# Two lent row slots with a continuous junction, and projections that begin with half of the modulation

## What is computed

```python
mod = silu(c) @ w_ada + b_ada                       # 1024 -> 6 * 1024
sh1, sc1, gt1, sh2, sc2, gt2 = split(mod, 6)
h = rms_norm(x, g_mix) * (1 + sc1) + sh1
q_sb, k_sb, v_sb, q_d, k_d, v_d, gate_sb, gate_d = split(h @ w_in)
# stick-breaking and dilated attention, their outputs gated and merged:
x = x + gt1 * (merged @ w_out)
h2 = rms_norm(x, g_ffn) * (1 + sc2) + sh2
# sparse feed-forward: 8 heads pick 16 of 16384 experts for each token
act = gelu(einsum('cd,ckd->ck', h2, peer_u[expert]))
x = x + gt2 * einsum('ck,ckd->cd', gate * act, peer_v[expert])
x = rms_norm(x, g_final)
# the second block follows: projections, spatial gating, attention, a dense feed-forward layer of 4096
```

## Time and profile before

| | us |
|---|---|
| three runs | 1466.15, 1467.89, 1471.02 |
| median | 1467.89 |
| the profiled execution | 1470.94 |
| its span | 1469.1 |
| PE busy in the span | 1312.6 (89%) |
| DVE busy | 777.3 (53%) |
| ACT busy | 331.3 (23%) |
| POOL busy | 296.4 (20%) |
| read from HBM | 516.89 MB |

### The profile page before, as it was taken

One profiled execution on the slowest core, in us unless ns is written; L12 is line 12 of the kernel. 1 busy time (PEld: TensorE's weight loads), 2 busy tenths in 40 slices (PEclk: granted clock), 3 DMA queues, 4 the chain that ended last, 5 costly groups with the idle time before them and its releaser, 6 DMA issues.

```text
span 1469.1 us, 14710 instructions
## 1 busy us (share of the span) xinstructions
PE 1312.6 (89%) x4900; PEld 748.0 (51%) x4900; DVE 777.3 (53%) x2083; ACT 331.3 (23%) x871; POOL 296.4 (20%) x275
## 2 busy tenths in 40 slices
PE   7999999698998897768888999898886899999997
PEld 6877995464655564334344543444332334554444
DVE  5146535576677677668756676575656522210002
ACT  1231223222221123233213212021110133411102
POOL 1000001333333334332313223232233000000000
PEclk7999999899999999998999999999999999999999
DMA  8966875899999999998999999999999899688882
GB/s 353 409 226 253 305 261 201 348 381 379 389 403 418 418 417 410 420 410 332 417 390 417 390 419 416 411 411 377 418 417 417 337 365 350 214 260 277 286 304 103
DMA packets 101594, 518.91 MB, mean 353 GB/s; under 512 B 11665, under 2 KB 12561, under 8 KB 66705
## 3 DMA queue, kind: packets, MB, share of 16 engines
q0 software_dynamic: 38592, 293.62, 49.0%
q1 hardware_dynamic: 61632, 220.43, 40.7%
q10 hardware_dynamic: 1296, 3.93, 0.7%
HBM read 516.89 MB, written 1.05 MB: 353 GB/s over the span
## 4 chain that ended last, share of the span: by engine, by line
PE 58%; DMA 29%; DVE 8%; ACT 3%; issue 2%; POOL 0%; DVEq 0%; ACTq 0%; POOLq 0%
PE ps_M L921 24%; DMA ring<-in_w_second 15%; DMA ring<-in_peer_uv,arena 8%; PE ps_T L718 7%; PE ps_T L719 6%; PE ps_M L450 5%; DMA ring<-in_w_pq 4%; PE ps_M L628 4%; DVE ring L1994 2%; PE ps_M L687 2%; PE ps_M L460 1%; PE ps_M L651 1%; DVE arena L1790 1%; PE ps_SA L687 1%; DMA arena<-in_w_ada 1%
## 5 line engine op out<-in xcount | busy, mean ns | idle before, releaser
L921 PE MATMUL ps_M<-ring,arena 128*128 128x512 f32 x1072 | 495.3, 601 | 39.8 <-DMA ring<-in_w_second 38.2
L921 PEld LDWEIGHTS ps_M<-ring,arena 128*128 128x128 f32 x1072 | 194.2, 190 | 288.9 <-issue 232.6
L1211 POOL DMA_INDIRECT ring<-in_peer_uv,arena x145 | 164.6, 1135 | 368.5 <-PE ps_T L719 324.6
L1211 POOL DMA_INDIRECT arena<-in_peer_uv,arena x111 | 124.8, 1124 | 328.3 <-PE ps_T L719 240.7
L718 PE MATMUL ps_T<-ring,arena 128*128 128x512 f32 x246 | 132.6, 621 | 36.9 <-ACT arena L1347 36.7
L1336 ACT ACTIVATE arena<-arena 128x2 f32<-128x2 f32 x128 | 26.0, 203 | 474.8 <-DVE arena L2014 471.3
L719 PE MATMUL ps_T<-ring,arena 128*128 128x512 f32 x246 | 129.2, 608 | 0.0
L718 PE MATMUL ps_T<-arena 128*128 128x512 f32 x190 | 100.0, 608 | 24.1 <-ACT arena L1347 24.1
L1994 DVE SCALAR_TENSOR_TENSOR ring<-ring,arena 128x1024 f32<-128x1024 f32 x72 | 87.6, 1220 | 58.4 <-DMA ring<-in_peer_uv,arena 58.1
L1994 DVE SCALAR_TENSOR_TENSOR ring<-ring,merged 128x1024 f32<-128x1024 f32 x73 | 89.1, 1221 | 48.2 <-DMA ring<-in_peer_uv,arena 48.1
L719 PE MATMUL ps_T<-arena 128*128 128x512 f32 x190 | 97.8, 596 | 0.0
(11 more groups left out here) (284 smaller groups left out, 1452.6 us busy)
## 6 DMA issues: line engine op xcount, KB each, us to landing
ring<-in_w_second SPq DMA_DIRECT2D x276, 512.0 KB, 4.5
ring<-in_w_in SPq DMA_DIRECT2D x70, 512.0 KB, 7.4
arena<-in_w_ada POOLq DMA_DIRECT2D x12, 2048.0 KB, 10.9
ring<-in_w_pq SPq DMA_DIRECT2D x30, 512.0 KB, 4.5
ring<-in_w_out SPq DMA_DIRECT2D x16, 512.0 KB, 4.8
ring<-in_w_br SPq DMA_DIRECT2D x16, 384.0 KB, 3.5
ring<-in_peer_uv,arena POOLq DMA_INDIRECT x145
arena<-in_rel SPq DMA_DIRECT2D x1, 2048.0 KB, 10.5
```

The source lines that it names most:

```text
L921: m = mm(bank, left[c], w[:, c, :], start=first and c == 0, stop=last and c == 1)
L1211: pool.indirect_dma_start(row_slots[n % PAIRS], None, A["peer_uv"], bass.IndirectOffsetOnAxis(ap=expert[:, u % 3, k:k + 1], axis=0))\
```

## The change

**Row slots.** tmp and merged are lent as row slots 3 and 4 to the gathers below 63 (`EARLY`); the ring pairs are slots 5 to 8. The order of slots is 0, 1, 2, 3, 4, 5, 7, 8, 6 below 63 and 0, 1, 2, 5, 7, 8, 6 from there on (`CYCLES`); each gather waits for the row that its slot held (`ROW_SLOT`). The tiles before the first turns are reordered (q0, ldv, lsv, q1), and PE does ldv's values, then the two gates ("lga", 0) and ("lgb", 0), then lsv's values, all before turn 0; ACT's takes and stick_soft1(0) move along, lsv's copy to turn 4.

**Junction.** `due(n)` goes on over row 127: rows 126 and 127 are accumulated in turns 128 and 129, and residual(0) follows these two turns. `LEAD` is 8. gate_expo and gate_norm of a head are done in turns 12 and 14 of the head before (head 0's before turn 0), and the product with the spatial mask moves from turn (7, 0) to (6, 13).

**Opening.** The chunks are loaded and worked in the order 0, 2, 1, 3 (`CHUNKS`). PE takes two blocks of chunks 0 and 2 and none of 1 and 3. The normalised tmp, the gain and hT are made in two halves of four feature pieces. The eight tiles of queries and keys are multiplied over the first four pieces of features (`stick_half(i, 0)`), and after chunks 1 and 3 over the other four; their sums stay in M0, M1, T0 and T1, two tiles in each, and ACT copies two tiles at once. SP loads tile 0 after chunk 0 has landed, tiles 1 and 2 after chunk 2, 3 to 5 after chunk 1, and the others after chunk 3.

The diff, without its unchanged lines but for the opening on DVE, and without five hunks (the count of the semaphores rows_in, waits of tile_shift moved by one, the two gates left out of phase -1 on PE and ACT, and the last weigh):

```diff
@@ -34,19 +34,25 @@
-OWN, VR = 3, 8
-PAIRS = OWN + VR // 2
+OWN, LENT, VR = 3, 2, 8
+ROW_SLOTS = OWN + LENT + VR // 2
+EARLY = 63
-BY_TENSOR = (2, 2, 1, 1) + 8 * (0,)
+BY_TENSOR = (2, 0, 2) + 9 * (0,)
+CHUNKS = (0, 2, 1, 3) + tuple(range(4, 12))
+NTH = {ch: n for n, ch in enumerate(CHUNKS)}
-FIRST = [(s, j) for lo in (0, 2) for j in (lo, lo + 1) for s in ("sq", "sk")]
+STICKS = [(s, j) for lo in (0, 2) for s in ("sq", "sk") for j in (lo, lo + 1)]
+FIRST = list(STICKS)
@@ -54,15 +60,15 @@
-FIRST += [("lsv", j) for j in range(SB_PAIRS)] + [("q0", half) for half in (0, 1)]
-FIRST += [("ldv", j) for j in range(4)] + [("q1", half) for half in (0, 1)]
+FIRST += [("q0", half) for half in (0, 1)] + [("ldv", j) for j in range(4)]
+FIRST += [("lsv", j) for j in range(SB_PAIRS)] + [("q1", half) for half in (0, 1)]
-LEAD = 6
+LEAD = 8
@@ -80,9 +86,7 @@
-    t = max(0, n - 1) // (NH * TOPK) if n == NU * TOPK else n // (NH * TOPK)
-    lo, hi = t * NH * TOPK, (t + 1) * NH * TOPK
-    return [r for r in ((n - LAG,) if n < hi else range(hi - LAG, hi)) if r >= lo]
+    return [n - LAG] if LAG <= n < NU * TOPK else list(range(n - LAG, n)) if n == NU * TOPK else []
@@ -91,6 +95,14 @@
+CYCLES = (0, 1, 2, 3, 4, 5, 7, 8, 6), (0, 1, 2, 5, 7, 8, 6)
+ROW_SLOT, landings = [], {s: [] for s in range(ROW_SLOTS)}
+for n in range(NU * TOPK):
+    s = CYCLES[0][n % 9] if n < EARLY else CYCLES[1][(n - EARLY) % 7]
+    ROW_SLOT.append((s, len(landings[s]) + 1, landings[s][-1] if landings[s] else None))
+    landings[s].append(n)
@@ -285,6 +297,7 @@
+        row_slots += [b[:, :, :].rearrange("p c t -> p (c t)") for b in (tmp, merged)]
@@ -400,13 +413,13 @@
-            return row_slots[n % PAIRS][:, 0:D]
+            return row_slots[ROW_SLOT[n][0]][:, 0:D]
-            return row_slots[n % PAIRS][:, D:2 * D]
+            return row_slots[ROW_SLOT[n][0]][:, D:2 * D]
-            return rows_in[n % PAIRS], 16 * (n // PAIRS + 1)
+            return rows_in[ROW_SLOT[n][0]], 16 * ROW_SLOT[n][1]
@@ -440,15 +453,28 @@
-            def both_tiles(name, fresh=False):
+            def both_tiles(name):
-                    if fresh:
-                        pe.wait_ge(h_norm1, c + 1)
+            def stick_half(i, half):
+                name, b, lo = STICKS[i], ("M0", "M1", "T0", "T1")[i // 2], i % 2 * T
+                if half == i % 2 == 0:
+                    claims[b] += 1
+                use[name] = (b, claims[b] - 1)
+                w = tile(name)
+                for c in range(4 * half, 4 * half + 4):
+                    if i == 0:
+                        pe.wait_ge(h_norm1, c + 1)
+                    m = mm(ps[b][:, lo:lo + T], w[:, c, :], hT[:, c, :], start=i % 2 == c == 0, stop=i % 2 == 1 and c == KC - 1)
+                if half == i % 2 == 1:
+                    finish(m, name)
@@ -463,16 +489,16 @@
-                bank = claim("S0" if ch in (0, 2, 10) else "S1", ("ada", ch))
+                bank = claim("S0" if ch in (0, 1, 10) else "S1", ("ada", ch))
-                pe.wait_ge(ada_ready, ch + 1)
+                pe.wait_ge(ada_ready, NTH[ch] + 1)
-                    m = mm(bank[:, b:b + 1], ada_sum[:, ch % 3, b * P:(b + 1) * P], ones[:, 0:1],
+                    m = mm(bank[:, b:b + 1], ada_sum[:, NTH[ch] % 3, b * P:(b + 1) * P], ones[:, 0:1],
@@ -750,16 +776,17 @@
-            for ch in range(4):
-                ada_columns(ch)
-            both_tiles(("sq", 0), fresh=True)
-            for name in (("sk", 0), ("sq", 1), ("sk", 1)):
-                both_tiles(name)
-            both_tiles(("sq", 2))
-            both_tiles(("sk", 2))
-            ada_columns(4)
-            both_tiles(("sq", 3))
-            both_tiles(("sk", 3))
+            ada_columns(0)
+            ada_columns(2)
+            for i in range(len(STICKS)):
+                stick_half(i, 0)
+                if i == 4:
+                    ada_columns(1)
+            ada_columns(3)
+            for i in range(len(STICKS)):
+                stick_half(i, 1)
+                if i == 5:
+                    ada_columns(4)
@@ -832,8 +859,11 @@
+            values(("ldvA", 1), 1, [("ldv", j) for j in range(4)])
+            for name in late_gates(-1)[0:2]:
+                tile_gate(1, name)
-            values(("ldvA", 1), 1, [("ldv", j) for j in range(4)])
@@ -891,8 +921,6 @@
-            for r in range(NH * TOPK - LAG, NH * TOPK):
-                accumulate(r)
@@ -1033,7 +1061,7 @@
-                    for n in range(3):
+                    for n in range(LAG + 3):
@@ -1153,8 +1181,14 @@
+            eng.wait_ge(ada_in[0], 16)
+            first_tiles(0, 1)
+            eng.wait_ge(ada_in[2], 16)
+            first_tiles(1, 3)
+            eng.wait_ge(ada_in[1], 16)
+            first_tiles(3, 6)
-            first_tiles(0, 12)
+            first_tiles(6, 12)
@@ -1186,7 +1220,7 @@
-            for ch in range(4):
+            for ch in CHUNKS[:4]:
@@ -1202,15 +1236,16 @@
-                if n >= PAIRS:
-                    pool.wait_ge(*row_taken(n - PAIRS))
-                elif n >= OWN:
-                    for slot in (2 * (n - OWN), 2 * (n - OWN) + 1):
+                s, _, held = ROW_SLOT[n]
+                if held is not None:
+                    pool.wait_ge(*row_taken(held))
+                elif s >= OWN + LENT:
+                    for slot in (2 * (s - OWN - LENT), 2 * (s - OWN - LENT) + 1):
-                pool.indirect_dma_start(row_slots[n % PAIRS], None, A["peer_uv"],
+                pool.indirect_dma_start(row_slots[s], None, A["peer_uv"],
-                    .then_inc(rows_in[n % PAIRS], 16)
+                    .then_inc(rows_in[s], 16)
@@ -1360,14 +1395,16 @@
-            act.wait_ge(scaled, 1)
+                if c % 4 == 0:
+                    act.wait_ge(scaled, c // 4 + 1)
-            def pair_take(j):
-                copy(("sq", j), qs[:, j, :])
-                copy(("sk", j), ks[:, j, :])
+            def stick_copy(i):
+                copy(STICKS[i], (qs, ks)[i // 2 % 2][:, i // 4 * 2:i // 4 * 2 + 2, :].rearrange("p j t -> p (j t)"), 2 * T)
@@ -1376,10 +1413,8 @@
-            pair_take(0)
-            pair_take(1)
-            pair_take(2)
-            pair_take(3)
+            for i in range(0, len(STICKS), 2):
+                stick_copy(i)
@@ -1427,15 +1462,18 @@
+            gate_expo(0)
+            stick_soft1(0)
+            copy(("ldvA", 1), vd[:, 1, 0:512], 512)
+            for s, (what, c) in enumerate(late_gates(-1)[0:2]):
+                gate_tile(1, s, c, (what, c))
-                if at == (-1, 1):
-                    stick_soft1(0)
+                if at == (-1, 4):
-                    copy(("ldvA", 1), vd[:, 1, 0:512], 512)
@@ -1508,8 +1546,8 @@
-                    if n % TOPK == 0:
-                        gate_expo(n // TOPK)
+                    if n % TOPK == 12 and n // TOPK + 1 < NU:
+                        gate_expo(n // TOPK + 1)
@@ -1517,8 +1555,6 @@
-            for r in range(NH * TOPK - LAG, NH * TOPK):
-                diagonal(r)
@@ -1719,6 +1755,8 @@
+                    for n in range(LAG):
+                        step()
@@ -1776,11 +1814,11 @@
-                a = ada_sum[:, ch % 3, lo:]
+                a = ada_sum[:, NTH[ch] % 3, lo:]
-                if ch >= 3:
-                    dve.wait_ge(mod_ready, ch - 2)
+                if NTH[ch] >= 3:
+                    dve.wait_ge(mod_ready, NTH[ch] - 2)
@@ -2030,17 +2068,32 @@
             ada_chunk(0)
             dve.wait_ge(*emptied("norm1"))
             V.reciprocal(rstd[:, :], rt[:, :]).then_inc(st.tick(), 1)
+            def norm_half(half):
+                cs = slice(4 * half, 4 * half + 4)
+                V.tensor_tensor(tmp[:, cs, :], xT[:, cs, :], rstd[:, :].unsqueeze(1).broadcast_to([P, 4, T]), ALU.mult)\
+                    .then_inc(st.tick(), 1)
+            def gain_half(half):
+                cs = slice(4 * half, 4 * half + 4)
+                own()
+                V.scalar_tensor_tensor(gain[:, 0, cs], mod[1][:, cs], 1.0, col["g_mix"][:, cs], ALU.add, ALU.mult)\
+                    .then_inc(scaled, 1)
+            ada_chunk(2)
+            own()
+            norm_half(0)
+            ada_bias(0)
+            ada_bias(2)
+            gain_half(0)
+            norm_half(1)
             ada_chunk(1)
-            own()
-            V.tensor_tensor(tmp[:, :, :], xT[:, :, :], rstd[:, :].unsqueeze(1).broadcast_to([P, KC, T]), ALU.mult)\
-                .then_inc(st.tick(), 1)
-            ada_bias(0)
-            ada_chunk(2)
             ada_bias(1)
             ada_chunk(3)
-            ada_bias(2)
             ada_bias(3)
-            V.scalar_tensor_tensor(gain[:, 0, :], mod[1], 1.0, col["g_mix"], ALU.add, ALU.mult).then_inc(scaled, 1)
+            gain_half(1)
             dve.wait_ge(const_in, 2 * 16)
             ada_chunk(4)
@@ -2094,6 +2147,7 @@
+            gate_norm(0)
@@ -2130,7 +2184,7 @@
-                elif at == (7, 0):
+                elif at == (6, 13):
@@ -2148,15 +2202,15 @@
```

(11 more changed lines are left out.)

4 lines of the change are left out of this document (2 added, 2 removed).

## The result

| | us |
|---|---|
| before, four runs | 1466.15 to 1471.02, median 1469.2 |
| after, four runs | 1447.73, 1448.63, 1451.98, 1453.85; median 1450.3 |
| ratio after to before, 95% interval | 0.9877 [0.9859, 0.9894] |
| span before and after | 1469.1 and 1450.1 |

A forecast was written before the change was run, and what follows sets the result against it. Bound by DMA bytes while the gathers lead, by PE matmuls before them and in the last third. -5 - 14 - 5.5 + 1 = -23.5 us from 1470.94 gave 1447.4; 3.05 lower for the median, 1444; range 1435 to 1456.

The forecast's parts named there:

- B: First rows of the gathers: nine row slots and earlier gates keep DMA from running dry; -14 us, ends 8 and 18.
- C: Junction after row 127: row slots come free sooner, leaving about 1 us of a 6.3 us DMA hole; -5.5 us.
- D: LEAD 8, two more turns ahead: gathers end two quarters earlier in the second block; +1 us (0 to 3.5).
- the signs that would have refuted A or B: DMA share from 240 to 430 under 0.97 though rows are ready (B); second halves starting after 50 us (A).
- A: Opening: PE's projections start at about 25.9, 10.5 earlier; second halves end at 62.5 against 67.72; -5 us.
- rival 2: Opening stays in series as before, through the bias wait or late tiles: A is 0, time 1449; chance 0.08.
- the most there is: DMA holes from 234 to 460 us: share 0.94 against 1.02, so 18 us at most to win.
- the check on PE: From 249 to 457 PE, busy 187.18 of 208 us, is near its limit; the hole at 340 to 360 won't close wholly.
- Both of its terms: D's terms: 1 MB less before the last row, -2.5 us; two quarters' matmuls after it, +3.6.
- Rival 1: Early rows given back: PE or ACT holds phases -1 to 2, B is 5, not 14; time 1453; chance 0.20.
- rival 4: No change, 1468: mean DMA rate (353 GB/s) at a ceiling, or slots still hold the fifth gather; chance 0.03.
- rival 5: Slower: two more rows in flight delay the tiles PE needs in turns 0 to 63; +33 us, 1477; chance 0.03.

## Why the prediction came out as it did

**The time** was 1444 with a range of 1435 to 1456, and is 1450.3. The forecast's own range of 1439 to 1450 just misses it. The parts behind the sum were off by more than the sum, and in both directions: B gave 5 us more than forecast, and C and D together took 4 or 5 where they should have given 4.5. That the sum still came within 6 us is in part luck. Neither of the signs that would have refuted A or B came: the share is 1.01 or more in each 20 us from 240 to 460, and the second halves start at 48.49 us, before 50.

**A, -5.** PE's first half starts at 25.27 us, as said (25.9). The second halves start at 48.49 instead of 47.3, and the stick scores at 64.85 instead of 63:

```profile
25.27 3.75 PE L475 MATMUL ps_M<-hT,ring 128*128 128x256 f32 x8 [1.30 <-ACT hT L1401]
29.21 6.33 PE L475 MATMUL ps_M<-hT,ring 128*128 128x256 f32 x24 [0.18 <-DMA ring<-in_w_in]
36.82 1.99 PE L475 MATMUL ps_T<-hT,ring 128*128 128x256 f32 x8 [1.28 <-DMA ring<-in_w_in]
...
48.49 7.26 PE L475 MATMUL ps_M<-hT,ring 128*128 128x256 f32 x32 [1.30 <-ACT hT L1401]
```

A gain of 3.65 instead of 5; the tiles are a little later than I had them (1.28 us of waiting), and the terms of that step add up to 47.0, not 47.3. The step that failed is the sentence that "all that follows to 214 us is PE work" and moves along: it does move along, but to a wait that stood still. Alone, 2.7 of the 3.4 us by which the first gather is earlier end at the gate tile. What rival 2 had for the opening ("A is 0") is what the opening alone gives, by another mechanism. In company it is worth 1.6 to 3.3, by ratios or medians.

**B, -14, is 18.8**, a little over the 18 that I called the most there is. The order was read rightly: the ninth gather is issued at 240.50 us,

```profile
240.50 1.77 POOL L1246 DMA_INDIRECT ring<-in_peer_uv,arena  x1 [2.19 <-PE ps_M L654]
```

with DMA at 1.01 or more from 240 on, and no idle of PE of 10 us before accumulation 4. What I mis-sized is the weight of the check on PE. I held that PE at 187 of 208 us would leave holes; in the changed kernel it is busy for 201.35 us of the same window of 208 and the hole of 340 to 360 is gone:

```profile
340.00:360.00 20.00, 18.36 (x70) 11.27 (x69) 15.32 (x53) 4.60 (x14) 5.17 (x6) 0.83 1.01 418
249.00:457.00 208.00, 201.35 (x895) 124.22 (x894) 153.50 (x473) 56.78 (x170) 77.89 (x68) 0.98 1.01 417
```

I read it so: nine slots let DMA run on while PE is short of rows in one turn and flooded in the next. With seven slots and the same order such holes are there (0.54 from 330 to 335 us).

**C, -5.5.** Row 128 gains 6.8 us over row 127 and row 136 still 5.3, the forecast's number. But POOL still waits 9.38 us, and two windows have a share of 0.80 and 0.72, where I expected no idle over 7 us and over 0.9 in each:

```profile
641.17 0.94 POOL L1246 DMA_INDIRECT arena<-in_peer_uv,arena  x1 [9.38 <-PE ps_T L745]
```

```profile
635.00:640.00 5.00, 2.85 (x4) 1.33 (x5) 4.79 (x19) 3.94 (x7) 0.00 (x0) 0.50 0.80 333
640.00:645.00 5.00, 5.00 (x13) 2.23 (x12) 4.86 (x14) 4.12 (x6) 1.90 (x2) 0.82 0.72 234
```

DVE is the engine that holds it, 4.79 and 4.86 of each 5 us: the residual stands behind rows 126 and 127 now, but still ahead of the routing and the normalised tile. The junction is shorter, not smooth; what of it reaches the end is between nothing and 5 us, as said above.

**D, +1, is the step that failed**: undoing it gives 8 us, and so does one addition moved with D left in place. Both of its terms were there. The quarters behind the last row were counted at their matmul time (3.6 us). The stretch grew by 7.7 us: those 3.6, 2.4 more of PE's waits for tiles that come through four ring slots (5.3 for 2.9), and 1.9 at the lower clock behind one of them. It shrank by 8.4 when D was undone (the six quarters that I expected behind the last accumulation are five, a wait, and the sixth). The 2.5 us for less weight ahead of the last row left out that the two turns also change which work of the second block meets which turn, and DVE's wait of 12.61 us at the residual then drained the row queue. Where that hole is closed, D costs about what I said: between the kernel with the later addition and the one that has the two edits together only D differs, and by it row 255 stands 1.4 us earlier, the last stretch is 4.1 us longer, and the time is 1.6 us longer by the ratios (with intervals that overlap). I had costed D from one end only, and no rival spoke of the turns' place among the quarters. Rival 1 gave about the right time for a wrong reason: the rows taken early weren't given back by PE or ACT in phases -1 to 2.

**The rate.** At 416 GB/s over the first 226 us of gathers, and 357 over a shorter span, no ceiling showed (rival 4's mean was 353). Nor did nine rows in flight starve PE of tiles (rival 5): a routing tile lands in 4.9 us, where it took 4.5.

## What to carry to other kernels

When a change starts a bound resource earlier, follow the gain to the next wait that doesn't move: here a gate tile swallowed 2.7 of a faster opening's 3.4 us, and nothing showed in the time. Work tied by hand to a count of steps changes partners everywhere when its start is shifted by two steps, so look for the longest waits of the shared engine far behind the edit, and try a piece of the work that frees buffers ahead of them; here one dot product was enough. An index that both kernels go through in the same order, such as the row number, makes a ledger that shows gain and loss in minutes, where the sums over stages hide them in each other.
